# An autoregressive decoder layer on one core: token rows turned ahead of the expert ranks, gate weights partly beside the ring, hidden rows turned ahead of the scatter, and the matrix engine's loop walked from a table

## The reference, cut to what matters

```
ada = silu(c) @ w_ada + b_ada            -> sh1, sc1, g1, sh2, sc2, g2
u   = x * (1 + sc1) + sh1 ; proj = u @ w_in ; mix = [HGRN2 heads, stick-breaking heads] @ w_o
x   = LayerNorm(ALPHA * x + g1 * mix)
u2  = x * (1 + sc2) + sh2
moe: group = argmax(u2 @ w_gr + b_gr); top-2 of the 8 experts of that group
     y = sum over the two experts of gate * ((silu(u2 @ w_gate[e]) * (u2 @ w_up[e])) @ w_down[e])
x   = LayerNorm(ALPHA * x + g2 * y)
```

## Time and profile before

| what | us |
|---|---|
| median of 3 runs | 1674.13 |
| range of those runs | 1673.41 to 1674.44 |
| the profiled execution's own time | 1675.62 |
| its span | 1673.6 |
| PE busy | 1527.3 (91%) |
| DVE busy | 558.7 (33%) |
| ACT busy | 190.0 (11%) |

### The profile page before, as it was taken

One profiled execution on the slowest core, in us unless ns is written; L12 is line 12 of the kernel. 1 busy time (PEld: TensorE's weight loads), 2 busy tenths in 40 slices (PEclk: granted clock), 3 DMA queues, 4 the chain that ended last, 5 costly groups with the idle time before them and its releaser, 6 DMA issues.

```text
span 1673.6 us, 24924 instructions
## 1 busy us (share of the span) xinstructions
PE 1527.3 (91%) x9665; PEld 928.7 (55%) x9665; DVE 558.7 (33%) x1013; ACT 190.0 (11%) x339; POOL 82.9 (5%) x153
## 2 busy tenths in 40 slices
PE   4799999999999999999977999999999998999974
PEld 0366766446777655777544555646555554554532
DVE  0101058712232443314560233232323323223236
ACT  0000012100010222210241000000000000000001
POOL 3000000000212000000000000000000000000000
PEclk8799999999999999999987999999999999999998
DMA  9995788875544445854596999999999999999992
GB/s 370 422 388 224 299 327 324 322 284 197 164 155 154 149 161 166 300 183 139 210 422 259 407 421 421 421 420 421 420 422 420 421 421 420 421 421 420 421 425 88
DMA packets 83449, 537.56 MB, mean 321 GB/s; under 512 B 11444, under 2 KB 11620, under 8 KB 24866
## 3 DMA queue, kind: packets, MB, share of 16 engines
q1 hardware_dynamic: 75634, 512.60, 76.6%
q0 software_dynamic: 7760, 24.18, 4.4%
HBM read 532.87 MB, written 11.80 MB: 325 GB/s over the span
## 4 chain that ended last, share of the span: by engine, by line
PE 72%; DMA 17%; DVE 5%; issue 3%; POOL 1%; ACT 1%; SPq 0%; DVEq 0%; POOLq 0%; ACTq 0%
PE ps L642 19%; PE ps L1158 15%; DMA ring<-w_up 13%; PE ps L943 7%; PE ps L1175 7%; PE ps L663 7%; PE ps L624 4%; DMA ring<-w_ada 2%; PE ps L1143 2%; DVE arena L2051 1%; PE ps L1111 1%; PE ps L1149 1%; PE ps L670 1%; PE ps L865 1%; DMA u_rows<-arena 1%
## 5 line engine op out<-in xcount | busy, mean ns | idle before, releaser
L1158 PE MATMUL ps<-ring,arena 128*64 128x256 f32 x3200 | 357.5, 382 | 13.8 <-issue 7.7
L1158 PEld LDWEIGHTS ps<-ring,arena 128*64 128x64 f32 x3200 | 268.2, 138 | 109.0 <-issue 26.3
L642 PE MATMUL ps<-arena,ring 128*128 128x288 f32 x1024 | 256.6, 409 | 0.0
L642 PEld LDWEIGHTS ps<-arena,ring 128*128 128x128 f32 x1024 | 191.9, 190 | 66.7 <-issue 15.4
L1175 PE MATMUL ps<-arena 128*64 128x512 f32 x800 | 180.0, 602 | 23.3 <-DVE arena L2061 23.3
L624 PE MATMUL ps<-ring,silu_c 128*32 128x512 f32 x768 | 103.5, 655 | 35.3 <-DMA ring<-w_ada 19.0
L1175 PEld LDWEIGHTS ps<-arena 128*64 128x64 f32 x800 | 66.7, 138 | 120.7 <-issue 94.0
L943 PE MATMUL ps<-arena,ring 128*128 128x288 f32 x512 | 125.5, 407 | 0.0
L2057 DVE TENSOR_TENSOR arena<-arena,ps 128x256 f32<-128x256 f32 x25 | 10.5, 421 | 331.8 <-PE ps L1158 331.8
L663 PE MATMUL ps<-ring,arena 128*128 128x512 f32 x256 | 115.5, 599 | 2.1 <-DVE arena L1606 2.1
L1143 PE MATMUL ps<-arena 64*128 64x512 f32 x384 | 101.9, 624 | 15.0 <-DVE arena L2051 14.9
(11 more groups left out here) (452 smaller groups left out, 1145.1 us busy)
## 6 DMA issues: line engine op xcount, KB each, us to landing
ring<-w_gate SPq DMA_DIRECT2D x100, 1024.0 KB, 19.2
ring<-w_up SPq DMA_DIRECT2D x100, 1024.0 KB, 22.9
arena<-w_down SPq DMA_DIRECT2D x100, 1024.0 KB, 17.7
ring<-w_ada SPq DMA_DIRECT2D x96, 1024.0 KB, 8.8
ring<-w_in SPq DMA_DIRECT2D x48, 1024.0 KB, 6.4
ring<-w_o SPq DMA_DIRECT2D x32, 512.0 KB, 6.8
ring<-cache_k SPq DMA_DIRECT2D x16, 512.0 KB, 4.2
ring<-cache_v SPq DMA_DIRECT2D x16, 512.0 KB, 4.2
```

What stands on the lines that cost most here:

```text
L642: last = mm(ps[:, bank, 0:T], w[:, P * t:P * (t + 1)], uT[:, t, :], start=(t == 0), stop=(t == KC - 1))
L1158: last = mm(ps[B * s:B * (s + 1), 2 + c // 4, 0:256], xgT[:, 4 * (c % 4) + t, :], ring[:, c, 512 * t + 256 * s:512 * t + 256 * (s + 1)], s ...
```

## The change

Four things are changed.

- *Turns.* Turns 0 to 6 come before the ranks, 7 to 11 right behind them. The ranks take four matmuls into one bank with a fourth column group for the counts (`both` gets a row of zeros). Turns 12, 13, 16, 17 come ahead of the matmuls that spread g2, turns 14, 15, 18, 19 behind them. The shift of x1 is cut in two; the half for the former goes ahead of the router's work on DVE, the other, with the samples' shift and the copy of g2, behind the plan. ACT's two exponentials and table load go behind copy 11.
- *Gate chunks.* Six of g2's 16 chunks (8, 9, 10, 13, 14, 15) are loaded to arena space that is free after the head norms (`g2_side`), issued after the last w_o chunk, and ten go through the ring. Expert 0's chunks are issued in the order 2 to 7, 0, 1, 8 to 11.
- *Hidden rows.* In a block `turn_hidden` comes right behind `turn_rows`, ahead of `turn_rest` and `combine`, into bank 2. `combine` uses banks 0, 1 and 3 as well, so it waits for x's copy before step 2, for one add before step 3, and PE for two adds before down. PE no longer waits for `keep_where`; gate_or_up's chunk 4 waits for the last add of the block before. In the last block combine comes behind up and `turn_hidden`. DVE's guess of the mean reads half of each row.
- *Turns without a block.* PE's loop skips its first `lead` = 41 - nblocks turns, not the last ones, and reads the block's number from a table `turns`, which DVE writes with the plan. The other engines' loops are as before.

```diff
+        g2_side = [area(at, D) for at in (16384, 18432, 26624, 20480, 22528, 24576)]
+        G2_RING, G2_SIDE = (*range(8), 11, 12), (8, 9, 10, 13, 14, 15)
+        TURN = [*range(12), 12, 13, 16, 17, 14, 15, 18, 19, *range(20, 24)]
         # SP
-            for t in range(KC):
-                put(used(N_G2 + t - SLOTS), t % SLOTS, w_ada[5, t])
+            sp.wait_ge(v_stored, 3 * 16)
+            sp.wait_ge(nm_dve, 2)
+            for k, w in enumerate(g2_side):
+                sp.dma_start(w, w_ada[5, G2_SIDE[k]]).then_inc(side_loaded[0], 16)
+            for k in range(10):
+                put(used(N_G2 + k - SLOTS), k % SLOTS, w_ada[5, G2_RING[k]])
-            for c in range(MOE_CHUNKS):
+            for c in (2, 3, 4, 5, 6, 7, 0, 1, 8, 9, 10, 11):
                 if c < SLOTS:
-                    sp.wait_ge(ring_used, used(N_END - SLOTS + c))
+                    sp.wait_ge(ring_used, used(N_G2 + (c if c >= 2 else SLOTS + c)))
         # PE
             pe.wait_ge(ss_dve, 5)
-            g2_chunks(range(10))
+            for t in range(13):
+                g2_chunk(t)
...
-            g2_chunks(range(10, KC))
+            for n in range(7):
+                turn_tokens(n, u2T)
             pe.wait_ge(rt_dve, 1)
+            rank = ps[:, 2, 0:4 * NE].rearrange("p (i e) -> p i e", e=NE)
+            mm(rank, causal[:, 0:P], both, start=True, stop=False)
             for i in range(3):
-                mm(ps[:, 2, NE * i:NE * (i + 1)], causal[:, 0:P], both[:, i, :], start=True, stop=(i == 0))
-                for k in range(i):
-                    mm(ps[:, 2, NE * i:NE * (i + 1)], ones[:], both[:, k, :], start=False, stop=(k == i - 1))
-            for i in range(3):
-                last = mm(ps[:, 3, 0:NE], ones[:], both[:, i, :], start=(i == 0), stop=(i == 2))
+                last = mm(rank[:, i + 1:4], ones[:], bc(both[:, i, :], 1, 3 - i), start=False, stop=(i == 2))
             last.then_inc(rt_pe, 1)
-            for n in range(8):
+            for n in range(7, 12):
                 turn_tokens(n, u2T)
+            g2_chunk(13)
             pe.wait_ge(rt_dve, 2)
...
-            for n in range(8, 12):
-                turn_tokens(n, u2T)
+            for t in (14, 15):
+                g2_chunk(t)
+            pe.wait_ge(x1_dve, 1)
+            for n in (12, 13, 16, 17):
+                turn_tokens(n, rT)
             pe.wait_ge(rows_copied, 6)
...
-            pe.wait_ge(x1_dve, 1)
-            for n in range(12, 20):
+            pe.wait_ge(x1_dve, 2)
+            for n in (14, 15, 18, 19):
                 turn_tokens(n, rT)
...
+            lead = pe.value_load(turns[0:1, NBLK:NBLK + 1], min_val=1, max_val=NBLK - 1)
-                pe.wait_ge(spread_ready, 1)
-            def combine(n):
+            def combine(n, turned):
+                pe.wait_ge(sum_dve, n * 5 + 1)
                 for j in range(5):
-                    pe.wait_ge(sum_dve, n * 5 + max(j, 1))
+                    if j == 2:
+                        pe.wait_ge(x_copied, turned)
+                    if j == 3:
+                        pe.wait_ge(sum_dve, n * 5 + 2)
-                            last = mm(ps[0:tn, ((7, 4), (5, 6))[j % 2][r], :], spread[rows, t0:t0 + tn],
+                            last = mm(ps[0:tn, ((7, 4), (5, 6), (0, 1), (7, 4))[j][r], :], spread[rows, t0:t0 + tn],
-            with pe.Fori(0, NBLK) as i:
-                with pe.If(i < last_block):
+            with pe.Fori(0, NBLK) as turn:
+                with pe.If(turn > lead - 1):
+                    i = pe.value_load(turns[0:1, bass.ds(turn, 1)], min_val=0, max_val=NBLK - 1)
                     pe.wait_ge(x_copied, i + 1)
                     for c in range(8):
+                        if c == 4:
+                            pe.wait_ge(sum_dve, i * 5 + 1)
                         gate_or_up(c, i)
                     turn_rows(i + 2)
+                    turn_hidden(i)
                     with pe.If(i < 1):
                         turn_rest()
                     with pe.If(i > 0):
-                        combine(i)
-                    turn_hidden(i)
+                        combine(i, i + 2)
+                        pe.wait_ge(sum_dve, i * 5 + 3)
+                    pe.wait_ge(hT_dve, i + 1)
                     for q in range(4):
             for c in range(8):
                 gate_or_up(c, last_block)
-                if c == 3:
-                    combine(last_block)
             turn_hidden(last_block)
+            combine(last_block, nblocks)
         # DVE
-            v.tensor_tensor(rT[:, :, 0:TP], rT[:, :, 0:TP], bc(ln1t[:, 1, :], 2, TP), ALU.add).then_inc(x1_dve, 1)
+            shift_x1(0)
...
+            v.tensor_scalar(turns[0:1, NBLK:NBLK + 1], cum[0:1, NE - 1:NE], -1.0, NBLK + 1.0, ALU.mult, ALU.add)
+            link(v.tensor_scalar(rta(1700, NBLK, parts=1), iotab[0:1, 0:NBLK], cum[0:1, NE - 1:NE], -(NBLK + 1.0), ALU.add, ALU.add))
+            v.tensor_scalar(turns[0:1, 0:NBLK], rta(1700, NBLK, parts=1), 0.0, None, ALU.max)
...
+            copy_rows_out(used(N_END - 1), 5, bg2[:])
+            v.tensor_tensor(samp1, rT[:, :, TP:T], bc(ln1t[:, 1, :], 2, TS), ALU.add)
+            shift_x1(1)
```

More of the change, by code:

```diff
@@ L208, in layer @@
         s0_loaded = [sem(f"s0_loaded{i}") for i in range(2)]
-        first_loaded = [sem(f"first_loaded{i}") for i in range(5)]
-        first_used, shift_dve, fix_pe, fix_act = (sem(n) for n in ("first_used", "shift_dve", "fix_pe", "fix_act"))
+        side_loaded = [sem(f"side_loaded{i}") for i in range(5)]
+        side_used, shift_dve, fix_pe, fix_act = (sem(n) for n in ("side_used", "shift_dve", "fix_pe", "fix_act"))
         pool_step, dve_step, act_step = sem("pool_step"), sem("dve_step"), sem("act_step")
@@ L265, in layer @@
         oneh = [rta(339 + 96 * k, 3, NG, NEG) for k in range(2)]
-        both = rta(531, 3, NE)
+        both = rta(531, 4, NE)
         nb = rta(755, NE)
@@ L298, in layer @@
         plan = sb("plan", [1, NB1 + 2], I32)
+        turns = rta(1926, NBLK + 1, parts=1).bitcast(I32)
         idxs = sb("idxs", [P, NB1], I32)
@@ L616, in _, with ada_step @@
             mm = nc.tensor.matmul
+            def ada_step(w, t):
+                for j in range(4):
+                    last = mm(ps[32 * j:32 * j + 32, 0, :], silu_c[:, t, :], w[:, 512 * j:512 * (j + 1)],
+                              start=(t == 0), stop=(t == KC - 1))
+                return last
             def ada_chunk(slot, is_loaded, t, freed):
@@ L622, in ada_chunk @@
                     pe.wait_ge(rows_copied, freed)
-                for j in range(4):
-                    last = mm(ps[32 * j:32 * j + 32, 0, :], silu_c[:, t, :], ring[:, slot, 512 * j:512 * (j + 1)],
-                              start=(t == 0), stop=(t == KC - 1))
-                last.then_inc(ring_used, 1)
+                ada_step(ring[:, slot, :], t).then_inc(ring_used, 1)
             def ada_turn(copied, freed):
@@ L1148, in combine @@
                             rows = slice(B * (q // 2), B * (q // 2 + 1))
-                            last = mm(ps[32 * q:32 * q + 32, 7, :], spread[rows, TP:T],
+                            last = mm(ps[32 * q:32 * q + 32, 3, :], spread[rows, TP:T],
                                       yout_s[rows, 512 * (q % 2):512 * (q % 2 + 1)], start=True, stop=True,
@@ L1430, in keep_x1 @@
                   ).then_inc(tt_act, 1)
-            for n in range(12, 20):
+            for n in TURN[12:20]:
                 keep_x1(n, moe_out[n // 4 - 3])
@@ L1929, in _ @@
             v.memset(lg, 0.0)
+            v.memset(both[:, 3, :], 0.0)
             v.memset(vm, 0.0)
@@ L1936, in _, with shift_x1 @@
             dve.wait_ge(u2_act, KC)
-            v.tensor_tensor(samp1, rT[:, :, TP:T], bc(ln1t[:, 1, :], 2, TS), ALU.add)
-            v.tensor_tensor(rT[:, :, 0:TP], rT[:, :, 0:TP], bc(ln1t[:, 1, :], 2, TP), ALU.add).then_inc(x1_dve, 1)
+            def shift_x1(half):
+                ms = slice(8 * half, 8 * half + 8)
+                v.tensor_tensor(rT[:, ms, 0:TP], rT[:, ms, 0:TP], bc(ln1t[:, 1, ms], 2, TP), ALU.add).then_inc(x1_dve, 1)
+            shift_x1(0)
             dve.wait_ge(rt_pe, 2)
@@ L2035, in keep_where @@
                 for i, (t0, tn) in enumerate(TILES):
-                    last = v.tensor_copy(where[:, :, t0:t0 + tn], ps[:, 4 + i, 0:4 * tn].rearrange("p (v t) -> p v t", v=4))
+                    last = v.tensor_copy(where[:, :, t0:t0 + tn],
+                                         ps[:, (3, 4, 7)[i], 0:4 * tn].rearrange("p (v t) -> p v t", v=4))
+                    if i == 0:
+                        last.then_inc(sum_dve, 1)
                 last.then_inc(spread_ready, 1)
+                dve.wait_ge(sum_dve, 6)
+                dve.wait_ge(spread_ready, 1)
             def add_up(n):
@@ L2085, in _ @@
                     v.tensor_tensor(yout[:, 0:512], ps[:, 5, :], g2h[:, 0:512], ALU.mult).then_inc(y_evac, 1)
+            hidden(last_block)
+            hidden_turned(last_block)
```

(6 more changed lines are left out.)

74 lines of the change are left out of this document (41 added, 33 removed).

## The result

| | before | after |
|---|---|---|
| median, us | 1674.21 | 1657.09 |
| lowest and highest, us | 1673.41, 1674.44 | 1656.33, 1658.26 |
| span of the profiled execution, us | 1673.6 | 1654.8 |
| block 0's first gate matmul at | 887.53 | 886.29 |

The change makes the kernel faster by 1.0%: the ratio is 0.9899, with a 95% interval of 0.9882 to 0.9916. The prediction said 1647.8, with a range up to 1656; the median is 9.3 above the one and 1.1 outside the other. The span should have lost 26.3 us and lost 18.8.

What follows compares the result with a forecast made beforehand. The prediction took the expert weight stream at the DMA limit to bound the second half. An earlier block 0 (8.5), a closed pause (7.5) and a shorter end (10.3) took 26.3 off the span: 1647.8 us, range 1638 to 1656.

Steps and rivals of the forecast that it cites:

- The chain of the router, turns, stores and gather: Ahead of block 0: last u2 store issues at 855.2, lands at 865, gathered rows arrive at 869.5.
- The other path, to the second copy of g2: Ahead of block 0: PE's x1 turns and g2 spreading, then ACT's copies, finished at 869.6.
- PE walks the 16 skipped turns, at 7.75 as before: Between the turned rows (870.6) and block 0: skipping takes PE 7.75 us, 0.48 a turn, until 878.4.
- The register load: PE's load of the block's number from the table ahead of block 0: between 0 and 1.4 us, taken as 0.6.
- The rival "slower": Skipped turns ahead of block 0 cost a fetch each, 3.3 us, 53 for 16; time 1693; chance 4%.
- The prediction's sentence that the trace disagrees with the Trainium skill's rule: On PE's skipped turns: 0.48 us each in the trace, against a rule that taken branches outside fetched pages stall.
- The rival of free skips: Skipped turns cost nothing ahead of block 0: 7.75 and 1.4 of half clock go; time 1638.6; chance 12%.
- that of slow landings: u2 stores (10.8) and gather (7.85) stay slow; block 0 starts 4.6 later than forecast; time 1652.4; chance 20%.
- The pause, 7.5: The weight stream's second pause, after block 0's start, closes: 7.5 us won, bounds 4.5 and 9.
- The end, 10.3: From up's last chunk landing in the last block to the span's end: 41.2 us instead of 51.5.
- The period: Later blocks: stream stays at 30.39 us a block; PE's own period falls from 29.4 to about 27.5.
- The sum: Whole kernel: 8.5 + 7.5 + 10.3 = 26.3 us off a span of 1673.6, giving 1647.3; median time 1647.8.

Runs made afterwards that it cites:

- e4_last: e3 with PE's loop running to NBLK again, so the skipped turns come behind the last block; 1650.8 us, ratio 0.9852.
- e1: The changed kernel with PE's loop begun at turn 8, so that 8 turns are skipped and not 16; 1646.7 us.
- e2: The changed kernel with PE's loop begun at turn `lead`, so none is skipped, block number still loaded from the table; 1644.91 us.
- e3: The changed kernel with PE's loop running from 0 to the last block's number, without skipped turns or table load; 1644.38 us, ratio 0.9816.
- e5: e3 with a loop of 16 skipped turns over one small instruction set ahead of PE's real loop; 1653.39 us.
- e15: e5 with 32 skipped turns over one small instruction instead of 16; 1662.81 us.
- e16: e5 with one register load from the table between the 16 skipped turns and the real loop; 1653.76 us.
- e17: e5 with 160 never-run matmuls as the body that the 16 turns skip, and no register load; 1659.62 us.
- e12: e3 with 20 unused matmuls on PE during the gather and 5 behind the turning of its rows; 1652.43 us, ratio 0.9878.
- e13: e3 with five unused matmuls on PE during the gather and one behind the turning of its rows; 1641.33 us, ratio 0.9804.
- e6_last56: e4_last with 16 more turns to skip behind the last block, 32 instead of 16; 1665.05 us.
- e10_turn: e3 with the first seven u2 turns put behind the rank matmuls again; 1646.54 us, ratio 0.9834.

## Why the prediction was wrong, by its own steps

- **The chain of the router, turns, stores and gather** was right, to 0.1 at the gather's landing, and partly by luck. The last store left 1.4 earlier (the prediction's terms for the last u2 copy add up to 854.5, not 854.9; it ended at 853.56) and took 8.76 (10 taken); the gather took 5.64, not the 3.3 of an idle stretch, and these misses cancel. The other path, to the second copy of g2, ended at 868.5 (869.6 forecast) and held nothing.
- **The step that failed: "PE walks the 16 skipped turns, at 7.75 as before".** With the load they took 14.78 instead of 8.35. With that the predicted start of 879.0 becomes 885.4; the turned rows were 0.9 later than forecast (half clock: 1.96 for turning them), which makes 886.3, and 886.29 was measured. The 7.75 was a gap in a trace, and the work in it had begun 4.3 us before the gap did, as the same trace shows. To this comes 3.4 for the first jump over the body, less 1.2 under the turning. The register load, taken at 0.6, measured 0.54.
- **The rival "slower"** priced a fetch at 3.3 us for each of 16 turns. A cost of that size is there (3.41, the first test), but once, so its condition of 2.1 us a turn was far off. The prediction's sentence that the trace disagrees with the Trainium skill's rule held for the kernel before, though its 0.48 came from the misread gap; in the changed kernel it held for 15 of the 16 jumps and not for the first. The rival of free skips was wrong outright; that of slow landings had the gather partly right, and its price of 4.6 was not paid.
- **The pause, 7.5.** It closed, as said (308 GB/s in the lowest stretch once the stream ran). From gate(0) to up's last landing 728.9 passed after; 734.6 was reckoned for before: 5.7 won. The term was mis-sized by 1.8, about what half clock did: 2.75 lost in gate(0) (16.55 against 13.8), not 1.4, and SP issued w_down's first chunk at 911.39, 25.1 after the start and not 23.7.
- **The end, 10.3.** Up's last landing to the end took 39.6 (41.2 forecast), so 11.9 won. Combine took 4.66 instead of 5.1, and the guess was out of the way. Down ended 14.65 after the landing, 15 forecast, and what follows it took 25.0 instead of 26.0.
- **The period.** 30.39 from the sixth block on (up's last chunk at 1037.83 and, 19 blocks later, at 1615.18); PE's own is 26.9 in the early blocks (27.5 forecast), and the stream's 421 GB/s is untouched.
- **The sum.** 1.24 + 5.7 + 11.9 = 18.8 off the span instead of 26.3. The start carries nearly all of the 7.5 missing. From gate(0) to the end 768.3 was forecast and 768.5 measured, but there luck helped: the pause gave 1.8 less and the end 1.6 more. The other 1.8 of the miss is in the step from span to median: the profiled execution lay 1.5 above its median before and 0.2 below it after.

The parts of the change by the spans: with the walk left at the end (e4_last, 1649.6) the first three would have won 24.0; the fourth, the walk ahead of block 0 with its table, gave 5.2 of that back (6.3 by medians). It is shown by e1 to e4 that the walk is what held block 0, by e5, e15 to e17 and the sequencer's rows what it consists of, and by e12 and e13 that the half clock is on the path. That the half clock explains just the 1.8 missing in the pause is argued from these, not shown in the changed kernel itself.

## What to carry to other kernels

A gap in a trace is a lower bound for the work that fills it: an engine whose array still has matmuls queued has already walked part of the way, so a cost that is to be moved is measured by doubling it in place, or read from the sequencer's own rows, not from its gap. Before optional turns are moved, look whether the loop can end at a register, which removes them. And when a start is won by an earlier order, ask what lands next (here expert 0, held off by the side loads) and what clock the first matmuls will get after the shorter or longer wait.

## What the runs showed of the hardware

- A skipped turn of a loop costs PE 0.745 us over a block's body (the changed kernel and e1_skip8), 0.748 over a single instruction (e5_short and e15_short32) and 0.742 at the loop's end (e4_last and e6_last56). It is four instructions of the sequencer, two of them compare-and-branch, of 0.21 to 0.22 us each. The Trainium skill (Advanced Engine Details and Errata, Control Flow Timing) gives a compare-and-branch about 108 ns. The trace disagrees for PE: it shows about twice that.
- The first of 16 jumps over a long body took 3.41 us (changed kernel) and 3.77 (e17_long), the others 0.22, with one load of instructions while it ran.
- 4.3 us of skipping lay under matmuls that were already queued (kernel before).
- PE's granted clock was 0.50 at the start of gate(0) after 3.8 us without work and the short turning behind them (e3_dyn), and 1.00 with 3.5 us of filler in that wait (e13_busy5). The filler made gate(0) 2.4 shorter and the stretch from there to the end about 3.1, though its results are unused.
- The last store of u2 rows and the gather took 14.7 us together beside a full weight queue (e3_dyn), and 11.1 when they came 7 us later and the queue was emptying (e10_turn).
